# Where the SwiGLU's inner layer starts in SBUF: 128 bytes past a multiple of 512 in place of 192

## What is computed

```
h = rmsnorm(x, g_ffn1[l]);  x = x + 0.5 * swiglu(h, w1_a[l], w3_a[l], w2_a[l])
h = rmsnorm(x, g_mix[l]);   p = h @ w_in[l]
# three branches (Fourier, short convolution, pooling), gated and summed to merged
x = x + merged @ w_o[l]
h = rmsnorm(x, g_ffn2[l]);  x = x + 0.5 * swiglu(h, w1_b[l], w3_b[l], w2_b[l])

def swiglu(h, w1, w3, w2):
    return (silu(h @ w1) * (h @ w3)) @ w2      # inner width 2816 = 22 tiles of 128
```

## Time and profile before

| | us |
|---|---|
| median of 3 runs | 2808.46 (2802.94 to 2809.16) |
| the profiled execution | 2803.92 |
| its span, first to last instruction | 2801.9 |
| second block (from about 750 us on) | about 2050 |
| matmuls with xf moving, weights stationary | 6336 |
| matmuls with xf moving, e stationary | 1056 |
| matmuls with g moving | 2496 |
| matmuls with xg moving | 2112 |

### The profile page before, as it was taken

One profiled execution on the slowest core, in us unless ns is written; L12 is line 12 of the kernel. 1 busy time (PEld: TensorE's weight loads), 2 busy tenths in 40 slices (PEclk: granted clock), 3 DMA queues, 4 the chain that ended last, 5 costly groups with the idle time before them and its releaser, 6 DMA issues.

```text
span 2801.9 us, 40254 instructions
## 1 busy us (share of the span) xinstructions
PE 2716.1 (97%) x15816; PEld 2181.3 (78%) x15816; DVE 1774.7 (63%) x2645; ACT 1092.5 (39%) x1586; POOL 416.2 (15%) x464
## 2 busy tenths in 40 slices
PE   9998999889699999999999999999999999999998
PEld 6576343333399998888889999899998888899997
DVE  6635232222787776665588777986777655787775
ACT  6832110100454444332354444554444233354443
POOL 3211000000021111101131110311101111221111
PEclk9999999999899999999999999999999999999999
DMA  5146999999465643332345564456542333365651
GB/s 214 45 175 263 420 420 420 420 420 421 141 181 166 173 136 100 103 101 94 100 124 168 167 172 136 114 164 176 158 136 89 94 94 106 98 172 142 176 158 60
DMA packets 138176, 505.65 MB, mean 180 GB/s; under 512 B 17025, under 2 KB 17537, under 8 KB 113153
## 3 DMA queue, kind: packets, MB, share of 16 engines
q1 hardware_dynamic: 101952, 422.36, 40.4%
q0 software_dynamic: 34688, 73.42, 12.8%
q10 hardware_dynamic: 1344, 7.23, 0.6%
HBM read 502.95 MB, written 4.19 MB: 181 GB/s over the span
## 4 chain that ended last, share of the span: by engine, by line
PE 73%; DMA 14%; DVE 5%; issue 4%; ACT 2%; POOL 1%; SPq 0%; DVEq 0%; ACTq 0%; POOLq 0%
PE bank L658 22%; PE bank L656 22%; PE bank L657 22%; DMA raw_more<-in_moe 4%; DMA raw<-in_moe 3%; PE bank L804 3%; DMA raw_over<-in_moe 3%; PE bank L839 2%; DVE w_lo L1875 1%; DMA sums<-in_w_b 1%; ACT w_hi L1272 1%; PE bank L662 1%; DMA raw<-in_w_b 1%; DVE ft L2289 0%; DMA x_rows<-x_tok 0%
## 5 line engine op out<-in xcount | busy, mean ns | idle before, releaser
L1875 DVE TENSOR_TENSOR w_lo<-raw,w_hi 128x1024 fp32r<-128x1024 f32 (+1 forms) x346 | 434.6, 1269 | 272.2 <-ACT w_hi L1272 265.7
L656 PE MATMUL bank<-xf_hi,w_lo 128*128 128x256 f32 x2112 | 590.1, 279 | 17.2 <-DVE w_lo L1875 9.6
L658 PE MATMUL bank<-xf_hi,w_hi 128*128 128x256 f32 x2112 | 585.3, 277 | 0.0
L657 PE MATMUL bank<-xf_lo,w_hi 128*128 128x256 f32 x2112 | 585.2, 277 | 0.0
L1272 ACT ACTIVATE w_hi<-raw 128x1024 fp32r<-128x1024 f32 (+1 forms) x356 | 366.0, 1039 | 273.9 <-PE bank L658 247.3
L656 PEld LDWEIGHTS bank<-xf_hi,w_lo 128*128 128x128 f32 x2112 | 397.6, 188 | 27.2 <-issue 14.1
L657 PEld LDWEIGHTS bank<-xf_lo,w_hi 128*128 128x128 f32 x2112 | 397.6, 188 | 2.4 <-issue 1.0
L658 PEld LDWEIGHTS bank<-xf_hi,w_hi 128*128 128x128 f32 x2112 | 397.4, 188 | 0.0
L658 PE MATMUL bank<-g_hi,w_hi 128*128 128x512 f32 x832 | 327.4, 394 | 0.0
L657 PE MATMUL bank<-g_lo,w_hi 128*128 128x512 f32 x832 | 326.2, 392 | 0.0
L656 PE MATMUL bank<-g_hi,w_lo 128*128 128x512 f32 x832 | 323.5, 389 | 0.3 <-DVE g_lo L2331 0.3
(11 more groups left out here) (367 smaller groups left out, 4549.0 us busy)
## 6 DMA issues: line engine op xcount, KB each, us to landing
raw_more<-in_moe SPq DMA_DIRECT2D x96, 1024.0 KB, 26.5
raw_over<-in_moe SPq DMA_DIRECT2D x48, 1024.0 KB, 27.4
raw<-in_w_a SPq DMA_DIRECT2D x77, 512.0 KB, 6.1
raw<-in_w_b SPq DMA_DIRECT2D x76, 512.0 KB, 6.3
raw<-in_w_in SPq DMA_DIRECT2D x73, 512.0 KB, 3.6
raw_top<-in_moe SPq DMA_DIRECT2D x24, 1024.0 KB, 27.9
raw<-in_moe SPq DMA_DIRECT2D x24, 1024.0 KB, 28.6
sums<-in_w_a POOLq DMA_DIRECT2D x88, 256.0 KB, 4.9
```

The lines of the kernel that those rows point to most:

```text
L656: e.matmul(out, a_lo, b_hi, start=start, stop=False, skip_group_check=partial)
L657: e.matmul(out, a_hi, b_lo, start=False, stop=False, skip_group_check=partial)
L658: return e.matmul(out, a_hi, b_hi, start=False, stop=stop, skip_group_check=partial)
L1875: e.tensor_tensor(lo, source_of(k), hi.bitcast(F32), ALU.subtract).then_inc(s["lo"], 1)
```

## The change

The pad of 16 floats (64 bytes) in front of g_hi and g_lo goes, and the pad behind them grows by as much. g_hi and g_lo, which lay 192 bytes past a multiple of 512, lie at 128, and everything behind them stays at its address. No instruction is added, removed or moved on any engine; only the addresses of g in them differ.

```
-        sb("pad_g", [P, 16])
         g_hi = sb("g_hi", [P, 8, T], F32R)
         g_lo = sb("g_lo", [P, 8, T], F32R)
-        sb("pad_late", [P, 112])
+        sb("pad_late", [P, 128])
```

## The result

| | before | after |
|---|---|---|
| median, us | 2803.01 (2801.26 to 2809.16, 5 runs) | 2818.34 (2816.38 to 2819.59, 5 runs) |
| ratio | | 1.0048, 95% interval 1.0037 to 1.0059 |
| profiled execution, us | 2803.92 | 2819.59 |
| its span, us | 2801.9 | 2817.8 |

The changed kernel is slower: the ratio says 0.48%, and 15.3 us lie between the medians. The forecast was a gain of 4.7 us. What happened is rival A. The prediction reckoned from a median of three runs, 2808.46; with two more it is 2803.01, so differences say more here than the times themselves.

What follows compares the result with a forecast made beforehand. The prediction took TensorE, busy 97% of the span, as the bound. Its terms, -5.7 - 0.2 + 1.0 + 0.2 = -4.7 us, took the median of 2808.5 to 2803.8 us, with a range of 2800 to 2821.

Steps and rivals of the forecast that it cites:

- rival A: xf behind g stretches falls to its slow speed, 117.7 for 113.3 ns: +16.9 us, +12.2 in all, 2820.7 us; chance 0.25.
- Main reading: In stretches with g, TensorE (PE) bounds and other engines have room, so time saved per matmul is saved at the end.
- Term 1: g as moving operand, 2496 matmuls: 226.67 in place of 228.96 ns each, as xg at 128 takes; -5.7 us.
- Term 2: g as stationary operand in time_spectra: 8.48 us a layer in place of 8.58; -0.2 us over two layers.
- Term 3: Step into a g stretch, mostly from xf in down_part and down_last: 0.03 us each, +1.0 us taken.
- Term 4: Step back from g at 128 to xf at 192: at most 0.01 us for each of 32, +0.2 us.
- the sum: The likeliest case, all terms together: -4.7 us, 2803.8 us, bounds -5.9 to -3.5; chance 0.60.
- point of decision: Share of the 32 g stretches with slow xf behind them from which rival A decides: 28% (4.7 of 16.9).
- until the next e stretch sets it right: Rival A's limit: the 120 xf matmuls behind each g stretch stay slow only until the next stretch with e.
- Rival B: Nothing happens: g's surplus belongs to something other than its position against 512, or only moves; 2808.5 us, chance 0.08.
- Rival C: More than the sum: steps cost nothing and g at 128 brings slow xf back to fast; 2801.7 us, chance 0.07.
- 13.6 us (the sum) or 14.1 us (A): Sign in the profile after: time of the 120 xf matmuls behind a g stretch, telling the sum from rival A.

## Why the prediction was wrong

Main reading (PE bounds, other engines don't). Right: in the stretches with g, PE is busy throughout before and after, and of their distances only xf's grew. Of the 15.8 us between the two profiled spans, the xf matmuls behind g cost 16.5; g's own give back 4.3 (2.6 in `down_part`, 1.0 in `down_last`, 0.7 in w_o), e and the rest of the mixer stages 0.2 each. The other 4.0 aren't shown to come from the change: 1.5 are in the first block, which has no g (the first xf matmul starts at 748.63 us in place of 747.09), and 2.5 at the starts of passes, where PE also waits for weights. Those starts differ by up to 1.4 us each between the kernel before and the one with g at 448 as well, so no cause is read from them.

Term 1, g moving at 226.67 ns. Right in its size, which went by the twin row: 33.32 us for 147, and 10.91 us for 48 with the step, as forecast (10.88 to 10.91).

Term 2, time_spectra. 0.06 us a layer in place of 0.10; too small to matter.

Term 3, the step into g. Right: 0.03 us.

Term 4, the step back into xf, is the one that failed. I forecast at most 0.01 us, by the row of e, +0.2 us in all, and the measured cost is 14.13 - 13.60 = 0.53 us per stretch, 16.5 us in all (31 of the 32 had been fast before). The step of the reasoning that failed is the choice of the nearest row. I took e because it is an equal pairing, 192/192, and hands on the fast speed. The row of xg into g was of the very pairing that the change makes, 128/128 at width 512, going to 192/128, and its uneven distances were the only sight of what such a stretch leaves behind. I listed it for rival A and then gave e's row more weight. Equal pairings don't leave equal rhythms; 192/192 at width 256 and 128/128 at width 512 differ in position and in width, and no run tells which of the two makes the difference.

Rival A was priced at +16.9 us for its own part, measured 16.5. In all it had +12.2 us; the medians differ by 15.3, and the ratio's interval is 10.4 to 16.5 us, so its sum holds. That its time of 2820.7 lies so near the measured 2818.3 is partly luck: it was reckoned from a median that is 5.5 us above the present one, and the loss is 3.1 us more than A's. The chance of 0.25 was too low. The bounds given for the sum, -5.9 to -3.5 us, were too narrow by their own terms: term 1 had nothing as one bound, with which they reach to +2.4; the loss lies outside even so. Its point of decision, 28% of the stretches, was passed by far: all 32 are slow. Its "until the next e stretch sets it right" held in the changed kernel, 32 times, and in several of the experiments it didn't.

Rival B is refuted by term 1. Rival C had it that g at 128 repairs slow xf; the opposite is so.

What the profile was to show served well: the line "13.6 us (the sum) or 14.1 us (A)" told the two cases apart at a glance.

On the Trainium skill's rule, quoted in the prediction, that weight loads take no read bandwidth from the running matmul (TensorE: Matmul & The Clock Gate, Part 2: What happens when you issue a matmul): seven positions of one moving operand gave four distances between 226.7 and 233.1 ns at the same shape and clock. So the runs disagree with what the prediction made of the rule, that position is free. Whether the weight loads take anything from the running matmul no run here shows, and the rule itself stays open.

## What to carry to other kernels

Before moving an operand for the sake of its own matmuls, look at what stands behind them: the rhythm that a stretch leaves can cost the next one more than the stretch gains, here 16.5 us against 4.3. When a trace shows the same matmul at two speeds without idle time between, find where it switches, at a stretch or at a late start, and keep the stretch that sets it right; and when you need the price of a step between two stretches, take the row of the same pairing and width, not that of the same outcome.

## What the runs showed of the hardware

- The distance between starts of fp32r matmuls with a weight load each depends on where the operands start in SBUF. At width 512, with weights at 128, it is 226.7 ns for the moving operand at 128, 228.9 at 192 and 448, 232.3 at 0 and 256, 233.1 at 64 and 320, all at a granted clock of 1.00, 2.4 GHz: positions 256 bytes apart are alike. For the stationary operand only 128 and 192 were seen: xf at 192 takes 120.0 ns with e at 192, and 113.3 or 117.8 with e at 128. (Positions are those past a multiple of 512.)
- At width 256, xf at 192 with weights at 128 has two steady speeds, 113.3 and 117.8 ns, and keeps the one that it is given, to the end of a pass where nothing stands against it. g at 192 hands it on. g at 0, 64, 128, 256 and 320 leave the slow one, 32 times in 32 each. In the kernel before it also went slow in the middle of a stretch, at two late starts (812 us).
- A stretch at 192/192 can restore the fast one. Behind g at 128 seven matmuls did it 32 times in 32, three and one did not. Length alone doesn't decide: 24 with e did it 32 times in 32 in the changed kernel, 16 times in 32 with g at 64 or 320, and never with g at 0 or 256 or behind the three more matmuls.
- What makes the rhythm inside the chip stays open. The traces show distances and not what TensorE waits for within one.
